# Gate slices of the HGRN2 layer unit by unit, and weight splits at other steps, in a two-layer decoder kernel

## The reference, cut to what matters

```
q_raw, f_raw, i_in, z = split(h @ w_in)          # 4 x 1024 columns
q = silu(q_raw);  f = lb + (1 - lb) * sigmoid(f_raw);  k = 1 - f;  v = i_in
# per head (8 heads of 128): a causal linear attention in which key s
# reaches query t damped by the product of f over s+1..t
o = o * rsqrt(mean(o * o) + eps) * g_norm         # per head
y = (o * silu(z)) @ w_out
x = x + y;  out = rmsnorm(x) * final_norm
```

## Time and profile before

| what | value |
|---|---|
| time, median of 3 runs | 331.47 us (331.27 to 331.49) |
| the profiled execution's own time | 331.14 us |
| its span, first to last instruction | 329.3 us |
| mean granted TensorE clock over the span | 0.995 |
| PE busy | 317.5 us, 96% of the span |
| DVE / ACT / POOL busy | 229.0 / 188.4 / 57.8 us |
| output projection's first slice starts | 300.69 us |

### The profile page before, as it was taken

How to read it: one execution, slowest core, us unless ns; L and a number is a source line. 1 busy time by engine, 2 the same in 40 slices (tenths; PEclk the granted TensorE clock), 3 DMA queues, 4 the chain that set the end, 5 groups by cost and what they waited for, 6 DMA issues and landing times.

```text
span 329.3 us, 6171 instructions
## 1 busy us (share of the span) xinstructions
PE 317.5 (96%) x2380; PEld 268.0 (81%) x2380; DVE 229.0 (70%) x400; ACT 188.4 (57%) x400; POOL 57.8 (18%) x55
## 2 busy tenths in 40 slices
PE   7999999998999999999999999999999999998993
PEld 6689778867989877777678878999999788897882
DVE  3977953649569978879928726277449988489824
ACT  4875255347686666668536706738445036898223
POOL 1004022070433443346300010100000011101000
PEclk9999999999999999999999999999999999999997
DMA  7999999616490920034270773653662434001011
GB/s 249 398 347 199 298 332 194 218 43 203 110 200 0 205 53 2 0 98 160 66 255 0 253 268 117 251 192 98 227 251 87 172 94 167 2 1 66 0 64 64
DMA packets 28685, 49.41 MB, mean 150 GB/s; under 512 B 3241, under 2 KB 7729, under 8 KB 28657
## 3 DMA queue, kind: packets, MB, share of 16 engines
q1 hardware_dynamic: 25616, 44.30, 42.8%
q10 hardware_dynamic: 2528, 2.69, 4.1%
q0 software_dynamic: 512, 2.03, 1.8%
HBM read 47.97 MB, written 1.05 MB: 149 GB/s over the span
## 4 chain that ended last, share of the span: by engine, by line
PE 72%; DVE 18%; ACT 5%; issue 2%; POOL 2%; ACTq 0%; DVEq 0%; POOLq 0%
PE bank L549 67%; DVE w_lo L1076 6%; ACT w_hi L827 3%; PE bank L728 3%; DVE nmax L1273 2%; POOL rp L1432 1%; DVE w_lo L1162 1%; PE bank L649 1%; PE bank L593 1%; DVE prob_t L1285 1%; DVE qk L1362 1%; DVE ft L1329 1%; DVE h_lo L1139 1%; DVE qk L1348 1%; DVE zT L1220 1%
## 5 line engine op out<-in xcount | busy, mean ns | idle before, releaser
L1076 DVE TENSOR_TENSOR w_lo<-raw,w_hi 128x1024 fp32r<-128x1024 f32 (+1 forms) x80 | 89.2, 1159 | 35.0 <-ACT w_hi L827 34.9
L549 PE MATMUL bank<-w_hi,h_hi 128*128 128x512 f32 x192 | 77.8, 411 | 1.8 <-DVE h_lo L1177 1.1
L549 PE MATMUL bank<-w_lo,h_hi 128*128 128x512 f32 x192 | 75.3, 392 | 0.3 <-DVE w_lo L1162 0.3
L549 PE MATMUL bank<-w_hi,h_lo 128*128 128x512 f32 x192 | 75.3, 392 | 0.0
L827 ACT ACTIVATE w_hi<-raw 128x1024 fp32r<-128x1024 f32 (+1 forms) x80 | 72.8, 965 | 2.1 <-issue 1.9
L549 PE MATMUL bank<-h_hi,w_hi 128*128 128x256 f32 x224 | 64.7, 289 | 0.0
L549 PE MATMUL bank<-h_hi,w_lo 128*128 128x256 f32 x224 | 63.3, 283 | 0.0
L549 PE MATMUL bank<-h_lo,w_hi 128*128 128x256 f32 x224 | 63.3, 283 | 0.0
L549 PEld LDWEIGHTS bank<-w_hi,h_hi 128*128 128x128 f32 x192 | 36.1, 188 | 11.1 <-issue 3.8
L549 PEld LDWEIGHTS bank<-h_hi,w_hi 128*128 128x128 f32 x224 | 42.9, 192 | 0.4 <-DVE w_lo L1076 0.2
L549 PEld LDWEIGHTS bank<-h_lo,w_hi 128*128 128x128 f32 x224 | 42.9, 192 | 0.3
(11 more groups left out here) (194 smaller groups left out, 422.3 us busy)
## 6 DMA issues: line engine op xcount, KB each, us to landing
raw<-in_hg SPq DMA_DIRECT2D x16, 1024.0 KB, 7.3
raw<-in_nsa SPq DMA_DIRECT2D x12, 1024.0 KB, 8.4
raw<-in_nsa_out SPq DMA_DIRECT2D x8, 512.0 KB, 8.2
raw<-in_hg_out SPq DMA_DIRECT2D x4, 1024.0 KB, 6.9
raw<-in_nsa SPq DMA_DIRECT2D x8, 256.0 KB, 5.2
w<-in_w1k SPq DMA_DIRECT2D x2, 1024.0 KB, 15.2
w<-in_w1v ACTq DMA_DIRECT2D x2, 1024.0 KB, 11.4
x_res<-in_x SPq DMA_DIRECT2D x2, 256.0 KB, 4.1
```

The lines of the kernel that those rows point to most:

```text
L549: return nc.tensor.matmul(o, lhsT, rhs, start=start, stop=stop, skip_group_check=True)
L1076: m = V.tensor_tensor(lo, src, hi.bitcast(F32), ALU.subtract)
```

## The change

Two tables are changed. `Z_ORDER` puts the gate slices of V_Z0 for both token tiles ahead of those of V_Z1 for tile 0. Before, the tile 0 slices of both units came first. TensorE executes the same forms at the same places. What changes is which weights twelve of the slices use: those at steps 255 to 282. V_Z0 is thereby finished at step 266 in place of 282. V_Z1 is first used at step 271 in place of 255, and ends at 289 as before.

`SPREAD` of V_Z1 and of V_O0 gets other numbers. Counted in steps:

| quarter | V_Z1 hi before | now | V_Z1 lo before | now | V_O0 hi before | now | V_O0 lo before | now |
|---|---|---|---|---|---|---|---|---|
| 0 | 242 | 250 | 243 | 251 | 282 | 272 | 283 | 273 |
| 1 | 242 | 255 | 243 | 256 | 285 | 277 | 286 | 278 |
| 2 | 254 | 260 | 254 | 261 | 285 | 280 | 286 | 281 |
| 3 | 254 | 265 | 254 | 266 | 285 | 282 | 286 | 283 |

```diff
-Z_ORDER = [(V_Z0, 0), (V_Z1, 0), (V_Z0, 1), (V_Z1, 1)]
+Z_ORDER = [(V_Z0, 0), (V_Z0, 1), (V_Z1, 0), (V_Z1, 1)]
...
-SPREAD = {... V_Z1: (4, 0, 44, 39), V_O0: (0, 3, 2, 2), ...}
+SPREAD = {... V_Z1: (12, 17, 22, 27), V_O0: (6, 11, 14, 16), ...}
```

More of the change, by code:

```diff
@@ L213, in split_count @@
     return kk + 1 if u == 0 else KT + NQ * (u - 1) + kk // 2 + 1
-SPREAD = {U_KW: (6, 7, 7, 0), U_Q0: (9, 5, 18, 15), U_Q1: (10, 13, 20, 26), U_Z0: (4, 0, 7, 12), U_Z1: (6, 7, 8, 12), U_O0: (17, 14, 28, 45), U_O1: (31, 47, 66, 93), V_V0: (0, 0, 1, 4), V_V1: (0, 0, 3, 6), V_F0: (0, 0, 11, 0), V_Q0: (2, 7, 20, 19), V_F1: (3, 5, 5, 6), V_Q1: (1, 0, 4, 9), V_Z0: (3, 5, 3, 5), V_Z1: (4, 0, 44, 39), V_O0: (0, 3, 2, 2), V_O1: (3, 1, 7, 4)}
+SPREAD = {U_KW: (6, 7, 7, 0), U_Q0: (9, 5, 18, 15), U_Q1: (10, 13, 20, 26), U_Z0: (4, 0, 7, 12), U_Z1: (6, 7, 8, 12), U_O0: (17, 14, 28, 45), U_O1: (31, 47, 66, 93), V_V0: (0, 0, 1, 4), V_V1: (0, 0, 3, 6), V_F0: (0, 0, 11, 0), V_Q0: (2, 7, 20, 19), V_F1: (3, 5, 5, 6), V_Q1: (1, 0, 4, 9), V_Z0: (3, 5, 3, 5), V_Z1: (12, 17, 22, 27), V_O0: (6, 11, 14, 16), V_O1: (3, 1, 7, 4)}
 GATED_LAG = 3
```

## The result

The changed kernel took 332.00 us, the median of 17 runs (331.36 to 332.25), where the kernel before took 331.36 in the same comparison (17 runs, 330.68 to 331.55). The ratio is 1.0019, 95% interval 1.0012 to 1.0027, or 0.64 us slower with 0.4 to 0.9. So the slowdown is clear of the noise, if small. The forecast was 0.85 slower, 332.3. The two profiled executions are 331.14 and 331.51 us, with spans of 329.3 and 329.7.

A forecast was written before the change was run, and what follows sets the result against it. TensorE, busy 96% of the span, was taken as the bound, so only its waits count. Lead -1.0, level waits +1.5, ScalarE +0.3, scaling +1.0, `h_lo` -1.1, V_O1 +0.15 gave +0.85 us, 332.3; range 330.6 to 333.3.

The forecast's parts named there:

- rival A: Whole kernel: the forecast itself, 0.85 us slower at 332.3 us, own range 331.8 to 332.9; chance 0.5.
- Lead of 1.0 in levels 1 and 2: Level 2: without the pair of low parts in front of level 1, TensorE gains 1.0 us.
- VectorE without a break, and two products on top: VectorE up to level 5's first update: four low parts in the chain, two GpSimd products adding 2.5 us, ending at 277.8.
- Waits at levels 5 and 6: TensorE before level 6: waits for VectorE's updates spend the lead of 1.0 us and lose 0.5 more.
- Four high parts on ScalarE: ScalarE around levels 6 and 7: V_O0's high parts delay level 7's end and the first value product, +0.3 us in the sum.
- The scaling late for `yT`: VectorE behind level 7: V_O0's low parts and a third GpSimd product make the transposes lose another 1.0 us.
- The wait for `h_lo` goes: First output slice: `h_lo` is ready at 300.3, in time, so TensorE's wait goes, -1.1 us in the sum.
- The first low part of V_O1 late: Output projection: V_O1's first low part is ready at 307.1 where TensorE would ask at 306.9, about 0.15 us.
- The assumption on the merge: VectorE in the levels: a masked merge isn't held by a GpSimd product, taken as 0, at most 0.4 us.
- Rival B: GpSimd's three products find gaps and cost VectorE nothing: 1.1 us faster, 330.4 us; chance 0.15.
- C: One of the two hurting meetings of GpSimd and VectorE is missed: within 0.4 us, 331.1 to 331.9; chance 0.23.
- D: ScalarE's level 6 drains come one more high part (1.0 us) late, holding TensorE at level 7: 333.3 us; chance 0.12.

The follow-up runs named there:

- e6: Changed kernel with V_Z1's high parts behind steps 239, 247, 260, 260 and low parts one step later, V_O0 as changed: 330.93 us, 0.9989 of the kernel before.
- e7: Changed kernel with V_O0's high parts in two pairs behind steps 280 and 284, V_Z1 as changed: 330.65 us, 0.9977 of the kernel before.
- e1: Changed kernel with GpSimd's gate product cut from 512 columns to 2 in each of four groups: 329.85 us, 0.9952 of the kernel before.
- e4: Changed kernel with V_Z1's quarters back in two pairs as in the kernel before, V_O0 as changed: 331.88 us, 1.0016 of the kernel before.
- e2: Kernel before with GpSimd's gate product cut from 512 columns to 2: 329.62 us, 0.9948 of the kernel before.
- e8: Changed kernel with V_Z1's high parts behind steps 239, 247, 260, 260 and V_O0's behind 280, 280, 284, 284: 328.85 us, 0.9928 of the kernel before.
- e3: Changed kernel with V_O0's high and low parts back at the steps of the kernel before, V_Z1 as changed: 331.59 us, 1.0009 of the kernel before.
- e5: Kernel before with in effect only the order of the gate slices changed, V_Z1's and V_O0's splits as before: 331.51 us, ratio 1.0000.

## Why the prediction was right, step by step

The sign and the mechanism held, and the size nearly so: +0.64 measured, +0.85 forecast, inside the 331.8 to 332.9 of rival A. By the prediction's own line of 0.2% (0.66 us) the result falls just short of "slower", which had 0.58, into "within", which had 0.26. The interval (0.12 to 0.27%) can't settle that, but it does settle the sign. By steps, positions counted from level 1:

1. *Lead of 1.0 in levels 1 and 2.* Right: level 3 starts 8.51 after level 1, before it was 9.56.
2. *VectorE without a break, and two products on top.* Right in kind, too long by 0.6 us. The first update of level 5 was forecast to end at 277.8, thus 22.3 after level 1. The pair that starts with it began at 275.92, so it ended near 277.1, 21.7 after. The mis-sized term is the price of a product, taken as 1.27 each. The low parts were longer by 0.66 (1.88 less 1.22) and 1.08 (2.30 less 1.22). The first product was asked for at 263.36, could start only when the update had ended at 264.5, and a masked merge passed beside it. It ended at 265.63, and the low part was due at 264.84: 0.79 of it was left. The second ended at 274.91, with 1.21 left when the low part was due at 273.70. So the part of the product that falls on VectorE's queue is what is left of it when VectorE's next instruction of that kind is due, less 0.13 in both, and not the whole. The rows of before say the same, and the prediction misread them. The held instructions ended 1.1 us after GpSimd, not one full duration (1.22), and the longest low part had lost 1.07, not 1.27. The second product lay only for 0.44 us in the idle 0.93, not "mostly", and cost the update 0.68, which TensorE didn't feel.
3. *Waits at levels 5 and 6.* 0.36 and 0.63 where 0.5 and 1.1 were forecast, by that same error. Level 6 starts 21.85 us after level 1, and did 21.90 before, where a loss of 0.4 was forecast. Its second half waits as forecast (a row of 2.26, before 2.06), so behind level 6 the loss is 0.15, forecast 0.5.
4. *Four high parts on ScalarE.* Right in place, too small in size: 0.3 us were forecast and 0.5 measured. Level 7 takes 2.22 us on TensorE (282.41 to 284.63) where it took 2.00; in e6, whose V_O0 splits are the same, a wait of 0.21 on ScalarE's drain is named in front of its last quarter. The value product comes 1.81 after it (286.44), where it came 1.50 after before. e7, whose V_O0 parts stand behind level 6's drains, has 2.01 and 1.50 again. Where TensorE comes early, the same parts cost 0.8 (e1, e4).
5. *The scaling late for `yT`.* From the value product to `yT` it is 9.83 us and was 9.08, so 0.75 more, where 1.0 was forecast; 0.50 of it is listed as a wait. The third meeting is there as forecast (product asked for at 288.65, low part of 2.31), at 1.09 and not 1.27.
6. *The wait for `h_lo` goes.* Right: `h_lo` starts at 298.43, more than 2 us ahead of the slice. The slice itself starts 0.25 later from level 1 than before, where 0.7 was forecast.
7. *The first low part of V_O1 late.* Forecast 0.15. The second output unit starts at 306.48, and the gaps between TensorE's hi by hi products in front of and behind it are 0.78 and 0.77 us, where they were 0.68 before: 0.2. The span from the first output slice on is 28.87 us and was 28.61.

The assumption on the merge (0 us) was right. Rival B did not happen: all three meetings cost VectorE time. e1 shows what B had in mind. Without the products the first output slice comes 1.75 us earlier from level 1 than before, where B had 1.4 for the same stretch; but 1.4 of such a gain is there in e2 too, without the change. C did not happen either, as no meeting was missed. D's mechanism, ScalarE late at level 7, is step 4's with more weight. It was priced at a whole high part more, and costs 0.2 more than step 4 had.

The sum from level 1 to the end of the span: -1.05 (lead) +0.99 (waits for `qk`) +1.47 (between level 6 and `yT`, 19.00 against 17.53) -1.17 (from `yT` to the slice: 4.56 against 5.73) +0.26 (V_O1) gives +0.5, and the medians are 0.64 apart. So the forecast of 0.85 is as close as it is in part by luck: it had 0.35 too much up to the end of level 6 and 0.25 too much for the third meeting, and 0.2 and 0.1 too little for ScalarE and V_O1.

## What to carry to other kernels

A queue that looks free is not free if another engine's instruction can hold it: read min and max of an instruction's durations, not only its idle time, because here such a wait was booked as busy on both sides. Spreading helper work evenly over a stretch in which a chain is paced by that engine lengthens the chain; put it where the engine would wait for its producer, in lumps if these are where the room is (e8 against the changed kernel: the same eight quarters, 1% apart). And when a change removes one wait and the time doesn't fall, test its halves apart: here each half spent its own gain, and each could be mended alone. The list of waits is a lower bound: ScalarE's 0.8 us in e1 stood there as 0.3.

## What was not expected of the hardware

*The start decides some of the scatter.* The profiled executions start level 1 anywhere from 255.35 (e3) to 256.01 (e1), with no edit ahead of it but to V_Z1's first splits. The difference is there from the first low part on, that is from the landing of the first weights. These are the kernel before, the changed kernel, e5 and e7:

```profile
6.66 0.69 DVE L1162 TENSOR_TENSOR w_lo<-raw,w_hi 128x512 fp32r<-128x512 f32 x1 [0.77 <-ACT w_hi L861]
```

```profile
6.52 0.69 DVE L1162 TENSOR_TENSOR w_lo<-raw,w_hi 128x512 fp32r<-128x512 f32 x1 [0.77 <-ACT w_hi L861]
```

```profile
7.04 0.69 DVE L1162 TENSOR_TENSOR w_lo<-raw,w_hi 128x512 fp32r<-128x512 f32 x1 [0.77 <-ACT w_hi L861]
```

```profile
6.34 0.69 DVE L1162 TENSOR_TENSOR w_lo<-raw,w_hi 128x512 fp32r<-128x512 f32 x1 [0.77 <-ACT w_hi L861]
```

6.34 to 7.04 against level 1 at 255.38 (e7) to 256.00 (e5): 0.70 at the start, 0.62 at level 1. That is as much as the effect of this change, and the whole times of one execution each would not have told the two kernels apart.

*Who is served first isn't settled.* In every meeting read, the wide products got in behind the one VectorE instruction that was running. The two-column product of e1, asked for at 273.82, did not: it is listed for 3.35 us, through a low part (273.64 to 274.86) and both updates of level 5, none of which took longer than usual. Two others of e1's short products, asked for at 263.96 and 288.12, got in behind the one update that was running.

```profile
273.82 3.35 POOL L1461 TENSOR_TENSOR z_hg<-z_hg,g_row 128x2 f32<-128x2 f32 x1 [8.68 <-ACT z_hg L970]
```

```profile
273.64 1.22 DVE L1076 TENSOR_TENSOR w_lo<-raw,w_hi 128x1024 fp32r<-128x1024 f32 x1
274.77 2.35 DVE L1362 TENSOR_TENSOR qk<-qk,ft 128x1024 f32<-128x1024 f32 x2
```

Nobody waited for it there, so it cost nothing. Why this one stayed behind three instructions of VectorE where all others stayed behind one was not tried and is open.
